# Hybrid encoder block on one core: softmax probabilities turned by VectorE through DRAM, and orders of their own for the mixer's first and last steps

## The reference, cut to what matters

```python
s = jnp.einsum('bnigrd,bnjgd->bngrij', qc, kb) * (d ** -0.5) - slopes * dist   # 8 heads, 2 key heads, 192 keys a tile
p = jax.nn.softmax(jnp.concatenate([s, sink], axis=-1), axis=-1)[..., :-1]
o_b = jnp.einsum('bngrij,bnjgd->bnigrd', p.astype(v.dtype), vb)
o_a = gla_chunked(q_a, k_a, v_a, log_a)          # gated linear attention, state carried over chunks of 64
h = x + jnp.concatenate([o_a, o_b], axis=-1) @ w_out
h = h + hier_moe(rms_norm(h, norm2_w))           # router: top group, then top 2 of its 8 experts
```

## Time and profile before

| what | value |
|---|---|
| time, median of 3 runs | 1745.45 us (1743.9 to 1746.3) |
| the profiled execution | 1747.92 us, of which the span of the trace is 1746.0 us |
| TensorE (PE) busy | 1679.8 us, 96% of the span |
| VectorE (DVE), ScalarE (ACT), GpSimd (POOL) busy | 719.6, 503.7, 528.8 us |
| the chain that ended last, share by engine | PE 81%, DMA 5%, issue 5%, DVE 4%, ACT 3%, POOL 2% |

### The profile page before, as it was taken

How to read it: one execution, slowest core, us unless ns; L and a number is a source line. 1 busy time by engine, 2 the same in 40 slices (tenths; PEclk the granted TensorE clock), 3 DMA queues, 4 the chain that set the end, 5 groups by cost and what they waited for, 6 DMA issues and landing times.

```text
span 1746.0 us, 31293 instructions
## 1 busy us (share of the span) xinstructions
PE 1679.8 (96%) x10900; PEld 1236.8 (71%) x10901; DVE 719.6 (41%) x1721; ACT 503.7 (29%) x1318; POOL 528.8 (30%) x621
## 2 busy tenths in 40 slices
PE   6899999999999999999978899999999999999996
PEld 5666666767667676666645778887778887878784
DVE  1344355444554445543556433323333333333332
ACT  0444434433344424444342211111112111111111
POOL 0010010101101010100110465655556556656554
PEclk9999999999999999999989999999999999999998
DMA  9521222112121122112233599989999999999994
GB/s 357 125 72 38 73 79 78 60 36 84 72 84 41 55 84 72 66 42 72 79 101 121 196 324 348 356 303 352 342 344 355 316 341 329 357 328 364 325 323 151
DMA packets 158598, 333.84 MB, mean 191 GB/s; under 512 B 25525, under 2 KB 45082, under 8 KB 158564
## 3 DMA queue, kind: packets, MB, share of 16 engines
q1 hardware_dynamic: 131348, 278.02, 46.0%
q0 software_dynamic: 26352, 55.27, 9.1%
q10 hardware_dynamic: 864, 0.10, 0.0%
HBM read 298.94 MB, written 63.70 MB: 208 GB/s over the span
## 4 chain that ended last, share of the span: by engine, by line
PE 81%; DMA 5%; issue 5%; DVE 4%; ACT 3%; POOL 2%; ACTq 0%; POOLq 0%; DVEq 0%
PE bank L329 15%; PE bank L323 15%; PE bank L351 12%; PE bank L1346 11%; PE bank L1351 9%; PE bank L1333 9%; DMA xg<-v_dram,idxm 2%; PE bank L318 2%; DMA h_dram<-sums_quarters,movec 2%; PE bank L501 1%; PE bank L1368 1%; POOL xg L1252 1%; PE bank L408 1%; ACT L1397 1%; PE bank L450 1%
## 5 line engine op out<-in xcount | busy, mean ns | idle before, releaser
L329 PE MATMUL bank<-uT,w_in_sb 128*128 128x128 f32 x2304 | 277.5, 279 | 2.3 <-DVE uT L677 2.3
L329 PEld LDWEIGHTS bank<-uT,w_in_sb 128*128 128x128 f32 x2304 | 268.6, 195 | 11.1 <-issue 8.9
L1333 PEld LDWEIGHTS bank<-xT,wts 128*128 128x128 f32 x2048 | 251.7, 193 | 25.1 <-issue 18.1
L1333 PE MATMUL bank<-xT,wts 128*128 128x128 f32 (+2 forms) x2048 | 256.4, 285 | 5.8 <-DVE xT L1431 2.1
L323 PE MATMUL bank<-w_in_sb,uT 128*128 128x512 f32 (+1 forms) x768 | 261.5, 494 | 0.0
L873 POOL TENSOR_SCALAR ss<-ss 128x1 f32<-128x1 f32 (+1 forms) x49 | 9.4, 192 | 803.3 <-ACT junk L601 432.7
L1346 PE MATMUL bank<-xT,wts 128*128 128x128 f32 (+2 forms) x2048 | 247.9, 282 | 0.0
L1346 PEld LDWEIGHTS bank<-xT,wts 128*128 128x128 f32 x2048 | 245.0, 191 | 0.0
L1351 PE MATMUL bank<-wts,hT 128*128 128x512 f32 x512 | 232.2, 597 | 0.0
L351 PE MATMUL bank<-w_out_sb,mixT 128*128 128x512 f32 x512 | 222.7, 593 | 1.5 <-ACT mixT L551 0.8
L1252 POOL DMA_INDIRECT xg<-v_dram,idxm x165 | 196.5, 1191 | 65.4 <-issue 31.0
(11 more groups left out here) (258 smaller groups left out, 1766.0 us busy)
## 6 DMA issues: line engine op xcount, KB each, us to landing
wts<-w_gate_in SPq DMA_DIRECT2D x32, 2048.0 KB, 11.9
wts<-w_up_in SPq DMA_DIRECT2D x32, 2048.0 KB, 10.8
wts<-w_down_in SPq DMA_DIRECT2D x32, 2048.0 KB
x_sb<-x_in SPq DMA_DIRECT2D x17, 512.0 KB, 3.6
xT_in<-x_t_in SPq DMA_DIRECT2D x17, 512.0 KB, 4.8
w_in_sb<-w_in_in SPq DMA_DIRECT2D x4, 2048.0 KB, 12.1
h_sb<-x_in SPq DMA_DIRECT2D x16, 512.0 KB, 3.3
h_dram<-h_sb SPq DMA_DIRECT2D x16, 512.0 KB, 2.6
```

Of the source, the lines that this page charges most:

```text
L329: m = pe.matmul(bk[name][0:hi - lo, col:col + P], w_in[:, k, lo:hi], uT[:, k, :], start=k == 0, stop=k == KD - 1)
L1333: m = pe.matmul(G[m_ % 2][:, 0:w], wg[:, k, m_ * P:(m_ + 1) * P], xT[:, k, 0:w], start=k == 0, stop=k == KD - 1)
```

## The change

- **Probabilities.** In steps 1 to 15 the 12 transposes on TensorE and the three copies on ScalarE are gone. VectorE writes the normalised probabilities in four column groups (`p4`) over one tile `ekg`, which now holds the decays `E`, `keT` and `g_t` side by side; SP stores it to `p_dram` in four DMAs, reads it back into `pT` (128 x 1536), and VectorE transposes `pT` in place. `ob` reads it through `pTcq` and `pTpq`. Two steps that overwrite `ekg` (the gate's Abs on ScalarE, `E[:, 1]` on VectorE) wait for the store. Step 16 keeps the old way. The router's sum moves behind `g`.
- **Start.** Three of the six constants are waited for first, the others with `late_consts`. ScalarE runs a one-column Square early. TensorE runs 12 matmuls of ones before its first wait, and 4 more after the first `xTa`. `qk` of tile 0 and 1 waits for `uT` in halves. Step 0 spreads tile 1's `uT` before the decays, and the `keT` transposes of tile 0 stand behind `qk` of tile 1.
- **End.** Steps 14 and 15 are written out. In step 15 (`closing`) the scores stand between the first and second half of `wo0`, the softmax goes ahead of the gates and the decayed keys, and tile 14's second half of h is added in step 16. In step 16 (`last`) tile 14 is turned, routed (into bank 5) and chosen late.

```diff
+    ekg = sb("decays_keys_gates", [P, 4 * QKA + VA])
+    p4 = ekg[:, :].rearrange("p (a r) -> p a r", a=4)
...
+        act.wait_ge(sem("filled"), 1)
+        act.activation(warm[:, :], ones[:, 0:1], ACT.Square)
...
-    FIRST, CONSTS, LATE, W_OUT = 6 * 16, 5 * 16, 4 * 16, 10 * 16
+    FIRST, CONSTS, LATE, W_OUT = 3 * 16, 5 * 16, 7 * 16, 10 * 16
...
+        if not isinstance(i, int) or 1 <= i < NT:
+            wait_apart(sp, rider, (sem("p_ready"), 2 * i), (sem("p_moved"), 80 * (i - 1)))
+            turned = scratch["p"].rearrange("(a j) (t r) -> t j a r", a=4, t=4)
+            for t in range(4):
+                sp.dma_start(turned[t], p4[t * TAIL:(t + 1) * TAIL, :, :]).then_inc(sem("p_moved"), 16)
         if not isinstance(i, int) or i >= 2:
             wait_apart(sp, rider, (sem("v2_ready"), i - 1))
             sp.dma_start(tile_rows(scratch["v2"], i - 2), h[:, par, :]).then_inc(sem("v2_stored"), 16)
+        if not isinstance(i, int) or 1 <= i < NT:
+            wait_apart(sp, rider, (sem("p_moved"), 80 * i - 16), (sem("ob_done"), 2 * (i - 1)))
+            sp.dma_start(pT[:, :], scratch["p"]).then_inc(sem("p_moved"), 16)
...
+        if isinstance(i, int) and i == 0:
+            transpose_x(0)
+            pe_warm(4)
...
+            if early == 1:
+                keys(0)
...
+        if closing:
+            wo(0, range(HA, KD))
+            scores()
+            wo(0, range(HA))
+            wo(1, (*range(HA, KD), *range(HA)))
+        elif last:
+            wo(0, range(HA))
+            router_sum(bank[5])
+            wo(1, range(HA))
...
+                dve.tensor_tensor(p4[:, :, 0:HB * TAIL].rearrange("p a (h j) -> p h a j", h=HB),
+                                  sc[:, :, CHUNK:].rearrange("p h (a j) -> p h a j", a=4),
+                                  rden.unsqueeze(2).unsqueeze(3).to_broadcast([P, HB, 4, TAIL]), ALU.mult)
...
+            wait(v_, sem("p_moved"), 80 * i)
+            dve.transpose(pT[:, :], pT[:, :]).then_inc(sem("pT_ready"), 3)
...
+        if closing:
+            softmax()
+            gates()
+            weigh_keys()
+            wait(v_, sem("xr_loaded"), 16 * i)
+            add_h(i - 1, 0, 1 - par)
```

More of the change, by code:

```diff
@@ L303, in bank_free, with pe_warm @@
         return []
+    def pe_warm(n):
+        for _ in range(n):
+            nc.tensor.matmul(bank[3][:, 0:P], ones[:, :], ones[:, :], start=True, stop=True)
     def pe_iter(pe, i, par):
@@ L397, in pe_iter @@
         if on("router"):
[L398 to L409, removed]
+            router(bk["router"])
         if on("pTp"):
@@ L416, in pe_iter @@
                 transposes(f"pTc{n}", lambda c: sc[:, 4 * n + c, CHUNK:], 4)
-        if runs(INDEX["router"], i):
-            wait(pe, sem("halves_ready"), i - 1)
-            pe.matmul(bk["router"][:, P:P + NR], halves[0:100, :], C["twice"][0:100, :], start=True, stop=True)\
-                .then_inc(sem("router_summed"), 1)
         if on("g"):
@@ L424, in pe_iter @@
             project("g", C_G, C_LR).then_inc(sem("g_done"), 1)
+        if runs(INDEX["router"], i):
+            router_sum(bk["router"])
         if on("og0") and on("og1"):
@@ L466, in pe_iter @@
             project("kv", S_VB, IN_W, col=P).then_inc(sem("kv_done"), 1)
-        last = isinstance(i, int) and i == NT
         if last:
@@ L473, in pe_iter @@
             transposes("mixAT", lambda c: qk[:, c * P:(c + 1) * P], 4)
+            router(bank[5])
         if on("qb"):
@@ L490, in pe_iter @@
             transpose_x(i + 1)
-        for n in range(2):
-            wo(n, range(HA) if last else (*range(HA, KD), *range(HA)))
-        for gg in range(2):
-            if on(f"s{2 * gg}") and on(f"s{2 * gg + 1}"):
-                wait(pe, sem("qbT_ready"), i + 1)
-                wait(pe, sem("kb_ready"), i + 1)
-                for m_ in range(2):
-                    for a in range(2):
-                        r = slice(64 * a, 64 * a + 64)
-                        m = pe.matmul(bk[f"s{2 * gg + a}"][:, m_ * WK:(m_ + 1) * WK], qbT[r, 2 * gg + m_, :], kb[r, gg, :],
-                                      start=True, stop=True)
-                        if m_ == 1:
-                            m.then_inc(sem("s_done"), 1)
-        if on("keT"):
-            wait(pe, sem("keT_ready"), i + 1)
-            transposes("keT", lambda c: keT[:, c * P:(c + 1) * P], 2)
+        if closing:
[7 more added lines that the diff above has]
+            wo(1, range(HA))
+        else:
+            for n in range(2):
+                wo(n, (*range(HA, KD), *range(HA)))
+            scores()
+        if runs(INDEX["keT"], i) and not (isinstance(i, int) and i == 0):
+            keys(i)
     BK = {name: bank[k % 8] for k, (name, _, _) in enumerate(JOBS)}
@@ L561, in act_iter @@
                 .then_inc(sem("kblr_taken"), 1)
-        if isinstance(i, int) and i == NT:
+        if last:
+            square_h(NT - 2, par)
             wait(act, sem("mixAT_done"), 1)
@@ L723, in dve_iter @@
                     .then_inc(sem("u2T_ready"), 1)
-        elif old2:
-            wait(v_, sem("h_quarters_loaded"), 64 * (i - 1))
-            turned = u2T[:, :, :].rearrange("p k q -> p (k q)")
-            dve.transpose(turned, turned).then_inc(sem("u2T_ready"), 2)
-            normalise_h(i - 2)
+            choose(v_, i - 3, 1)
+        elif old2 and not last:
+            turn_h()
         if old:
@@ L794, in dve_iter @@
                 dve.tensor_tensor(mixA[:, :], mixA[:, :], gm[:, :], ALU.mult).then_inc(sem("mixA_ready"), 1)
+        if last:
+            turn_h()
+            choose(v_, i - 3, 0)
+            choose(v_, i - 3, 1)
+            take_logits(bank[5])
         if new:
@@ L862, in dve_iter @@
             dve.tensor_scalar(nm, m_, -1.0, None, ALU.mult).then_inc(sem("nm_ready"), 1)
+        if closing:
+            softmax()
[3 more added lines that the diff above has]
+            add_h(i - 1, 0, 1 - par)
+        else:
+            if new:
+                weigh_keys()
+            if old:
+                wait(v_, sem("xr_loaded"), 16 * i)
+                for n in range(2):
+                    if old2 and not (last and n == 1):
+                        if n == 0:
+                            v_.wait_ge(sem("logits_ready"), i - 1)
+                        choose(v_, i - 2, n)
+                    add_h(i - 1, n, 1 - par)
+            if new:
+                gates()
+                softmax()
     def pool_iter(po, i, par):
@@ L875, in rstd @@
             pool.tensor_tensor(dst, src, neghalf[:, 0:width], ALU.pow).then_inc(sem(done), 1)
-        late = 0 if isinstance(i, int) and i == NT else 1
+        late = {NT - 1: 0, NT: -2}.get(i, 1) if isinstance(i, int) else 1
         def rstd_x(t, x_step):
```

214 lines of the change are left out of this document (151 added, 63 removed).

## The result

The changed kernel takes 1715.1 us (median of 4 runs, 1711.2 to 1717.6) against 1744.7 for the kernel before (4 runs, 1743.7 to 1746.3): ratio 0.983, 95% interval 0.981 to 0.985, some 30 us faster. The forecast was 1701, its range 1695 to 1712. The profiled execution took 1716.39 us, its span 1714.6.

What follows compares the result with a forecast made beforehand. TensorE alone was taken to bound the mixer's steady steps. Gains of 20.4 (steps), 13.7 (last tile) and 10.3 (start) sum to 44.4 us, taking 1745.45 to 1701 us, range 1695 to 1712.

Steps and rivals of the forecast that it cites:

- their order is not touched, so they should only start earlier: Experts, from 940 us on, run from the routed tokens: expected only to start earlier, with no term in the sum.
- Steps 2 to 15: Mixer's steady steps: removing 12 transposes from TensorE frees 1.46 us in each of 14 steps, 20.4 us.
- The start: Up to tile 0's `ob`: earlier first projections and a filled 6.19 us hole, 10.3 us including step 1's transposes.
- the first probabilities' route: Tile 0's probabilities, written at 67.2, go out to DRAM and back in 7.9 us, before a 1.8 us transpose.
- one of the signs: At the start, `qb` of tile 0 was to be seen waiting for its weights.
- The 3.5 us of idle time ahead of `ob`: At the start, TensorE was to wait some 3.5 us for tile 0's turned probabilities before the first `ob`.
- The slow clock that was charged at nothing: Behind the first `ob`'s wait a slow clock could cost 2 us; charged nothing, 2 kept for the range.
- The last tile: Mixer's end: step 15's scores 10.4 us earlier and the reordered work behind them gain 13.7 us, bounds 10.4 to 15.
- The late case: Rival: turned probabilities a little late, each of 14 steps losing 1 us at 12.4 us of route: 1715; chance 0.12.
- Does not do what it says: Rival on the start: warming matmuls don't raise the clock, or the hole only moves behind `ob`: 1703 to 1705; chance 0.05.

Runs made afterwards that it cites:

- after_again: The changed kernel, unchanged, measured again as an anchor for other runs: ratio 0.981 to the kernel before.
- after_third: The changed kernel, unchanged, measured once more as an anchor for a later run: ratio 0.982 to the kernel before.
- E2: Not a run: an expert of the kernel's expert loop, numbered from zero; the first that is 160 columns wide.
- E6: Not a run: an expert of the kernel's expert loop, numbered from zero; the second that is 160 columns wide.
- before_narrow32: The kernel before, with 1 of the routing's 15 clock-keeping matmuls replaced by 9 narrow ones: 1756.3 us against 1745.3, ratio 1.006.
- start_both: The changed kernel with two step 1 edits, attention masks ahead of the probabilities and spare rows cleared behind the mix moves: ratio 0.983 to the kernel before.
- scores_late: The changed kernel with step 15's scores behind both halves of the output product again: ratio 0.988 to the kernel before.
- E1: Not a run: an expert of the kernel's expert loop, numbered from zero.
- narrow192: The changed kernel with 8 of the routing's 15 clock-keeping matmuls replaced by 56 narrow ones, moving the expert loop's code 192 instructions: ratio 0.986 to the kernel before.
- before_pad33: The kernel before, with 66 already satisfied waits (33 instructions) on TensorE between mixer and routing: ratio 1.007 to the kernel before.

## Why the prediction was wrong

- **The step that failed: "their order is not touched, so they should only start earlier".** Routing and experts stood in the sum at nothing. Their order and data are untouched, and yet the part behind the last sum took 6.5 us more in the profiled execution, and 3.9 and 3.2 more in the traces of after_again and after_third. TensorE stands ahead of E2 and E6 and runs at the lower clock behind some of these waits. That the place of the code decides, in the main, where it waits is shown: before_narrow32 loses 11 us by a move of 32 instructions, and the table goes by the place in 18 of 19 profiles. That the wait is a fetch of code is inferred from the packets. Half of the miss in this trace; without it the time would have been some 1709, inside the range.
- **Steps 2 to 15.** Mechanism right: steps without a wait, the route 9.97 us from written to landed (608.88 to 618.85) against 8.4 forecast, margin 2.2 against 3. The size was off: 1.27 a step for 1.46, because a row of the chain was taken for what its removal frees. 2.7 us.
- **The start.** The term that was too small is the first probabilities' route: 10.6 us (68.06 to 78.62) for 7.9, and they were written 0.9 us later than forecast. Together 3.6 of the 3.7 us. `qk` began at 11.86 as forecast (12.0), but took 9.2 us instead of 7.3; `qb` came 3.3 us sooner and not 4.0, and did not wait for its weights, as one of the signs had it. The 3.5 us of idle time ahead of `ob` appeared as 2.75 ahead of `g`, which the forecast had overlooked. The slow clock that was charged at nothing did come: behind the wait ahead of `g`, where `pT` covered it, and at 2.6 us in start_both, where the wait stands ahead of `ob`.
- **The last tile.** Right: 13.5 of 13.7, confirmed by scores_late.
- **The rivals.** The late case did not come: no step waits for `pT`. (The prediction gives its limit once as 11.4 us and once as just under 12; the 9.97 measured are under both.) "Does not do what it says" came in part. None was about the part behind the mixer, and the range had no room for it, though waits of 1.84 us at E1 and 0.38 at E2 could be read in the trace of before.

## What to carry to other kernels

Adding or moving code on one engine moves the rest of its program; where a loop with branches follows, count a few microseconds either way, and look at idle time released by "issue" together with packets on the instruction queue. To price work that is removed, take the distance from its first start to the start of what follows, not the row of the chain. A wait on TensorE is not over when it ends: behind 18 of the 28 waits for "issue" of over 2 us ahead of an expert the group that followed took another 1.4 us or more, mostly 1.7, at the lower clock level; behind the other ten nothing was lost.

## What was unexpected of the hardware

- Waits for "issue" of 1.7 to 4.5 us on TensorE with a packet of 16 KB of code ahead of or within each, all in the first nine experts; 11 us for a move of 32 instructions (before_narrow32), 6 to 10 us for one of 192 (narrow192).
- A satisfied wait is not free: 446 of them held TensorE for 23.85 us, 0.05 us each.
- Executions of the changed kernel spread by up to 10 us (1708.5 to 1718.8), those of before_pad33 by 14.5, where the kernel before spread by 3 to 8. What differs between them, and why TensorE waits again at E6 for a body that ran at E2, stays open.
